# Moving the summing of the last gate rows of the first MLP from the fourth to the fifth weight slot, and the next layer's rows of that quarter into slots five to eight

## The reference

```python
def _modulate(x, c, g, w, b):
    m = (c @ w + b)[:, None, :]
    shift, scale, gate = jnp.split(m, 3, axis=-1)
    h = _rmsnorm(x, g) * (1.0 + scale) + shift
    return h, 1.0 + gate
def _sq_relu_mlp(h, w1, w2):
    a = jax.nn.relu(h @ w1)
    return (a * a) @ w2
...
        h, gate = _modulate(x, c, norm_g[i, 1], ada_w[i, 1], ada_b[i, 1])
        x = x + gate * _sq_relu_mlp(h, mlp_w1[i], mlp_w2[i])
```

## Time and profile before

| | us |
|---|---|
| median of 3 runs | 1282.16 |
| the 3 runs | 1280.72, 1282.16, 1289.22 |
| the profiled execution | 1277.51 |
| its span, first to last instruction | 1275.8 |
| PE, DVE, ACT, POOL busy | 1239.8, 757.4, 447.0, 81.9 |
| mean granted clock of TensorE | 0.988 of full |

### The profile page before, as it was taken

The page is one execution under the profiler, slowest core; times in us unless marked ns, Lnnn a source line. Parts: engine busy times, 40 slices in busy tenths (PEclk is TensorE's granted clock), DMA queues, the critical chain, the costliest instruction groups (busy, mean ns, idle before and its releaser), DMA issues.

```text
span 1275.8 us, 16139 instructions
## 1 busy us (share of the span) xinstructions
PE 1239.8 (97%) x6260; PEld 1006.0 (79%) x6260; DVE 757.4 (59%) x1035; ACT 447.0 (35%) x609; POOL 81.9 (6%) x122
## 2 busy tenths in 40 slices
PE   6999999899999999999999999999999999999999
PEld 4789888688888888888779885568788888888887
DVE  8998968654645645565478957854743343443432
ACT  5543424312312313223442257862431231321321
POOL 0010000000000000060000001214000000000022
PEclk9999999899999999999999999999999999999999
DMA  9558780735453445422223320003133323223311
GB/s 325 189 132 244 279 303 22 271 120 169 174 173 127 169 165 173 173 75 67 89 77 100 99 66 2 1 2 99 57 109 99 99 99 91 78 99 94 99 66 66
DMA packets 132692, 157.48 MB, mean 123 GB/s; under 512 B 19784, under 2 KB 113152, under 8 KB 132608
## 3 DMA queue, kind: packets, MB, share of 16 engines
q1 hardware_dynamic: 125328, 153.82, 36.2%
q10 hardware_dynamic: 7312, 2.96, 1.0%
HBM read 151.39 MB, written 4.19 MB: 122 GB/s over the span
## 4 chain that ended last, share of the span: by engine, by line
PE 88%; DVE 5%; DMA 3%; ACT 2%; issue 1%; ACTq 1%; POOL 0%; SPq 0%; DVEq 0%
PE psum L1677 86%; PE psum L1681 2%; DMA w_raw<-in_mlp_w 1%; DVE work L1325 1%; DMA ada_first<-in_ada_w 1%; DVE h_lo L1335 1%; DVE w_lo L1311 1%; DMA raw_bn<-in_ssm_b_im 1%; ACT w_hi L769 1%; DVE ada_acc_c L1479 1%; ACT pT L1050 1%; ACTq L890 0%; DMA toep<-kr 0%; ACT h_hi L816 0%; ACT xT L783 0%
## 5 line engine op out<-in xcount | busy, mean ns | idle before, releaser
L1677 PE MATMUL psum<-h_hi,w_hi 128*128 128x512 f32 (+1 forms) x872 | 342.8, 393 | 4.0 <-DVE w_lo L1311 3.0
L1677 PE MATMUL psum<-h_lo,w_hi 128*128 128x512 f32 (+1 forms) x872 | 340.2, 390 | 0.0
L1677 PE MATMUL psum<-h_hi,w_lo 128*128 128x512 f32 (+1 forms) x872 | 340.0, 390 | 0.0
L769 ACT ACTIVATE w_hi<-w_raw 128x2048 fp32r<-128x2048 f32 x92 | 174.4, 1896 | 314.7 <-PE psum L1677 301.7
L1311 DVE TENSOR_TENSOR w_lo<-w_raw,w_hi 128x2048 fp32r<-128x2048 f32 x92 | 213.4, 2319 | 107.3 <-ACT w_hi L769 106.8
L1677 PE MATMUL psum<-a_hi,w_hi 128*128 128x512 f32 x512 | 203.4, 397 | 0.0
L1677 PE MATMUL psum<-a_lo,w_hi 128*128 128x512 f32 x512 | 203.0, 397 | 0.0
L1677 PE MATMUL psum<-a_hi,w_lo 128*128 128x512 f32 x512 | 203.0, 396 | 0.0
L1677 PEld LDWEIGHTS psum<-h_hi,w_hi 128*128 128x128 f32 (+1 forms) x872 | 163.6, 188 | 43.2 <-issue 6.8
L1677 PEld LDWEIGHTS psum<-h_hi,w_lo 128*128 128x128 f32 (+1 forms) x872 | 163.7, 188 | 34.8
L1677 PEld LDWEIGHTS psum<-h_lo,w_hi 128*128 128x128 f32 (+1 forms) x872 | 163.8, 188 | 33.6
(11 more groups left out here) (304 smaller groups left out, 1310.2 us busy)
## 6 DMA issues: line engine op xcount, KB each, us to landing
w_raw<-in_mlp_w SPq DMA_DIRECT2D x64, 1024.0 KB, 5.5
ada_l_ring<-in_ada_w SPq DMA_DIRECT2D x64, 384.0 KB, 6.1
w_raw<-in_cd_w_in SPq DMA_DIRECT2D x14, 1024.0 KB, 4.9
ada_ring<-in_ada_w SPq DMA_DIRECT2D x17, 384.0 KB, 5.1
ada_more<-in_ada_w SPq DMA_DIRECT2D x15, 384.0 KB, 4.6
ada_first<-in_ada_w SPq DMA_DIRECT2D x5, 1024.0 KB, 15.0
w_raw<-in_ab_w_in SPq DMA_DIRECT2D x4, 1024.0 KB, 8.1
w_raw<-in_ab_w_out SPq DMA_DIRECT2D x4, 1024.0 KB, 7.9
```

What stands on the lines that cost most here:

```text
L769: act.activation(w_hi[n % 2][:, :, 0:w], raw[n % 2][:, :, 0:w], ACT.Copy).then_inc(hi_ready, 1)
L1677: return nc.tensor.matmul(o, lhsT, rhs, start=start, stop=stop, **kw)
```

## The change

It reorders work in the first quarter of layer 0's MLP and touches one more place.

- DVE: late rows 0 to 2 are summed in the second step, 3 and 4 in the third, 5 to 7 in the fifth. Each waits only for the row before it. No layer 1 row is summed in the first four steps; they follow in the fifth (e0 to e2), sixth (e3 to e7), seventh (e8 to e11) and eighth (e12 to e15).
- PE: the sum of the late rows stands behind slot five, that of e0 to e7 behind slot six. The sum of e8 to e15 stays behind slot eight.
- DVE collects the late sum in the sixth step ahead of its residuals (tiles 2 and 3) and adds 1 to gate columns 2 to 7 there. For columns 0 and 1, which come from an earlier unit, that is done by an instruction in the output projection ahead of the MLP.
- SP: late rows 3 and 4 are issued behind load 4 (were behind load 3), rows 5 to 7 behind load 5 (were behind load 4). The waits are for the same buffers; their `ada_used` values are counted for the new order.

In quarters two to four all orders stay, and no work is added or removed but one DVE instruction on two columns.

```diff
-    LATE_STEPS = {1: range(0, 2), 2: range(2, 5), 3: range(5, 8)}
-    late_done = [43, 44, 47, 48, 49, 52, 53, 54]
+    LATE_STEPS = {1: range(0, 3), 2: range(3, 5), 4: range(5, 8)}
+    ROWS_Q0 = {4: range(0, 3), 5: range(3, 8), 6: range(8, 12), 7: range(12, 16)}
...
-                sp.wait_ge(ada_used, late_done[j - ADA_RING])
+                sp.wait_ge(ada_used, LATE_FROM + j - ADA_RING + 1)
...
-                    for j in {0: range(0, 3), 2: range(3, 5), 3: range(5, 8)}.get(i, ()):
+                    for j in {0: range(0, 3), 3: range(3, 5), 4: range(5, 8)}.get(i, ()):
                         late_row(j)
...
-        def ada_gate(a, parts):
+        def ada_gate(a, parts, k0=0, k1=KC):
             dve.wait_ge(mods_part, parts)
-            own(dve.tensor_scalar(mods[:, a, 16:24], mods[:, a, 16:24], 1.0, None, A))
+            g_ = mods[:, a, 16 + k0:16 + k1]
+            own(dve.tensor_scalar(g_, g_, 1.0, None, A))
             settle()
...
                     if i == 3:
                         ada_scale(1, 7)
+                        ada_gate(1, 7, 0, 2)
...
-                            dve.wait_ge(ada_used, late_done[j] - 1)
+                            dve.wait_ge(ada_used, LATE_FROM + j)
...
-                        dve.wait_ge(ada_used, late_done[j])
                 if layer == 0:
-                    for r in range(2):
-                        e = 2 * i + r
+                    for e in (ROWS_Q0.get(i, ()) if first else (2 * i, 2 * i + 1)):
...
+                if first and i == 5:
+                    ada_collect(7)
+                    ada_gate(1, 8, 2)
...
-                if first and i == 3:
-                    ada_collect(7)
-                    ada_gate(1, 8)
-                if layer == 0 and i % 4 == 3:
-                    s = i // 4
+                if layer == 0 and i in ((5, 7) if first else (3, 7)):
+                    s = i // 6 if first else i // 4
...
-                if first and i == 3:
-                    ada_sums(ADA_EARLY + late_done[7], 7)
-                if layer == 0 and i % 4 == 3:
-                    ada_sums(2 * ADA_STEPS + 8 * (i // 4 + 1) + 16 * q, 8 + i // 4 + 2 * q, q,
-                             7 if first and i == 3 else None)
+                if first and i == 4:
+                    ada_sums(ADA_EARLY + LATE_FROM + 8, 7)
+                if layer == 0 and i in ((5, 7) if first else (3, 7)):
+                    s = i // 6 if first else i // 4
+                    ada_sums(2 * ADA_STEPS + 8 * (s + 1) + 16 * q, 8 + s + 2 * q, q)
```

More of the change, by code:

```diff
@@ L1481, in quarter @@
                         ins.then_inc(ada_used, 1)
-                        dve.wait_ge(ada_used, late_done[j])
                 if layer == 0:
-                    for r in range(2):
-                        e = 2 * i + r
+                    for e in (ROWS_Q0.get(i, ()) if first else (2 * i, 2 * i + 1)):
                         k = e % 8
-                        dve.wait_ge(ada_l1[i], 32 * q + 32)
+                        dve.wait_ge(ada_l1[e // 2], 32 * q + 32)
                         src = ada_l1_ring[:, e, :]
@@ L1491, in quarter @@
                         else:
-                            late = sum(len(v_) for i_, v_ in LATE_STEPS.items() if i_ <= i) if first else 8
-                            dve.wait_ge(ada_used, LATE_FROM + late + e + 16 * q)
+                            dve.wait_ge(ada_used, LATE_FROM + 8 + e + 16 * q)
                             ins = dve.scalar_tensor_tensor(out=ada_acc[:, :], in0=src,
```

## The result

The changed kernel is faster. In the first comparison its median is 1266.61 us (4 runs, 1263.21 to 1268.57) against 1281.44 us (4 runs), ratio 0.9871 with a 95% interval of [0.9829, 0.9914]. More runs gave 1266.14 us against 1279.38 us, ratio 0.9906 [0.9888, 0.9924]: 12.0 us of 1279.38, interval 9.7 to 14.3. The forecast was 1271.3 us and 10.8 us, ratio 0.9916. It lies just outside the first interval and inside the second. The sign and the mechanism of the wait came as forecast; the size was 10% low against the 12.0 us, and 27% low against the 14.8 us between the first two medians. Left out of all ratios are runs more than 1.5% above the fastest of their kernel: 1294.86 and 1296.38 us of before, 1288.81 us of SP's order alone and 2484.01 us, of unknown cause, of the changed kernel with SP's order of before.

What follows compares the result with a forecast made beforehand. PE, busy 97% of the span, was taken as the bound, stopping for the last late row. Wait 5.90, sums 2.61 and slow start 2.31 us made 10.82 us: 1282.16 - 10.8 = 1271.3 us, range 1266 to 1276.5.

Steps and rivals of the forecast that it cites:

- PE's sum: PE in quarter one: the closing sum starts at 291.99 instead of 302.81, 10.82 us earlier, if every input is on time.
- Slot five's weights, and slot six's: SP's queue: load 5 issued at 220.7 instead of 236.4; load 6 near 231.6, with 6.8 us to spare.
- The spares at the sums: DVE's rows ahead of PE's three sums, behind slots five, six and eight, end 2.3, 2.1 and 2.5 us early.
- Rival A: A small wait comes back at PE's new sums; gain between 10.8 and 5 us, 1274 us; chance 0.11.
- Rival B: The reorder does not free slot five's weights; gain 3.4 to 8 us, 1276 us; chance 0.06.
- Rival C: DVE's rows take twice as long, about 2.05 us each in crowded steps; slower, 1284 us; chance 0.03.
- The price of the stop: PE between slots four and five: wait 5.90 us, slow sums 2.61 us, slow start of slot five 2.31 us.
- The offset of 4.65 us: Whole program: the runs' median lies 4.65 us above the profiled execution, taken as the same after the change.
- The clock part: PE behind the stop: full clock returns 2.61 us on the two sums and 2.31 us on slots five to eight.

Runs made afterwards that it cites:

- e0, e1: Not a run: a layer 1 row, which the changed kernel's DVE sums in the fifth step of the first quarter.
- e3: Not a run: a layer 1 row, which the changed kernel's DVE sums in the sixth step of the first quarter.
- e7: Not a run: a layer 1 row, the last that the changed kernel's DVE sums in the sixth step of the first quarter.
- e15: Not a run: a layer 1 row, the last that the changed kernel's DVE sums in the eighth step of the first quarter.
- sp_only: Kernel before with only SP's queue order changed, DVE and PE keeping their order, both sums adjacent behind slot four; ratio 0.991 and 0.9907 to before.
- before_filled_long: Kernel before with 36 unused identity products on PE filling the stop ahead of the late sum; ratio 0.9987 to before.

## Why the prediction was right or wrong

- **PE's sum.** Right. 79.99 us from slot two to the closing sum was forecast (291.99 - 212.00), 80.11 and 80.12 were measured.
- **Slot five's weights, and slot six's.** Right and on the safe side. Load 5 was issued at 217.95, 7.1 us behind the start of slot two, where 8.7 were forecast: without e0 and e1 DVE freed the late rows' buffers sooner. Load 6 went 19.1 us behind that start, 19.6 forecast.
- **The spares at the sums.** Right. The last late row ends at 249.20 + 3.26 = 252.46, PE's sum starts at 254.88: 2.4 us (2.3 forecast). Rows e3 to e7 end at 264.81, 2.56 us ahead of 267.37 (2.1 forecast), and e12 to e15 at 284.27 + 4.38 = 288.65, 2.4 us ahead of 291.01 (2.5 forecast). Rival A, a small wait at the new sums, did not come.
- **Rival B** fell with `sp_only`: the reorder frees the weights, and by itself it removes the wait.
- **Rival C** fell: a row took 1.10 us (5.51 / 5).
- **The price of the stop: the term that was mis-sized.** 90.81 us was taken as the stage of before, and with it 5.90 us for the wait. Four profiles have 90.81 to 92.88, mean 91.91, and waits of 5.74 to 7.79, mean 6.87 where the forecast's own execution has 5.74. The step that failed is the one that took 6.63 us for slot five's weights and 7.79 us for slot four's, the quickest of four landings each (means 7.29 and 8.26), as the kernel's own, and gave the range nothing for the other side. It treated the scatter of the runs as noise around a fixed gain, when part of it belonged to the stop that the change removes: the stage of before spreads over 2.07 us, that of the changed kernel repeats to 0.01 us in two profiles. With the mean the forecast would have been 11.8 us, 1270.4 us, which is 1.0 us of the 4.7 us by which the time was missed.
- **The offset of 4.65 us: the larger part of the miss in the time.** It was taken from a median of three runs and carried over unchanged. The 22 runs of before in the second comparison have a median of 1279.38 us, 1.87 us above the profiled execution; single ones spread from 1275.53 to 1284.44 us, with the mean clock between 0.992 and 0.982. So 2.8 us of the 4.7 (1271.3 against 1266.6) lie in that anchor, and the remaining 0.9 us is within the scatter. The anchor is itself uncertain: the later comparisons have 1282.39 and 1279.65 us for before. The profiled execution of after, 1268.57 us, was the slowest of its four.
- **The clock part.** Right in amount, 2.61 + 2.31 us, and in that the stop lowered the clock; incomplete in its cause. Taking the stop away would not have been enough: `sp_only` has no stop and loses 1.7 and 3.1 us to the clock, and `before_filled_long` shows 2.8 of the 4.9 us to be the idle time's. That the whole amount came is luck in part: the change also sets the two sums apart, which the prediction did not count on.

That the interval of the second comparison (9.7 to 14.3 us) holds the mean stage's 11.8 us settles the size well enough; the 14.8 us between the first two medians is within its interval (11.0 to 21.9 us of 1281.44); no run shows a cause for the 3.0 us beyond the stage. Not settled is why the landing of one megabyte differs by 1.3 us between executions, and whether the change has an effect on how long the clock stays low at later norms (3.4 or 6.8 us where it fell near 568 us).

## What to carry to other kernels

Where a queue issues in program order, put no transfer that waits for a buffer ahead of one that is free to go; changing that order alone took away the whole wait here. When a change removes a wait for a transfer, don't price it from one profile: its length differed by 2 us between executions here, and the change gains the mean and not the value that was seen. Where the clock matters, keep short one-column products of PE apart from each other by a block of full matmuls.

## What the runs showed of the hardware that was not expected

Two groups of six one-column float32 products back to back, 2.5 us in which PE counts as busy all the time, were followed by 1.2 GHz in the three profiles without idle time ahead of or between them, at a cost of 1.6 to 3.1 us, and in the one with only 0.36 us between them; one group alone, 1.25 us, in none of 86 (8 in this stretch, 78 later). A row of the same length at the norm was followed by it in 12 of 13 profiles. Filling a stop with identity products held 2.4 GHz while they ran (1.00 over 8 us) and brought 1.7 us of stage (90.18 against the mean of 91.91), since the two groups that followed lost the clock anyway. A 1 MB weight transfer with two or three 384 KB transfers issued just ahead of it took 6.63 to 8.65 us from issue to landing in the seven profiles with SP's order of before; the median of all 64 transfers of MLP weights on the page of before is 5.5 us.
